# Weight sums of a seven-product matrix multiply: from GpSimd instructions to accumulating DMAs, with the products in another order

## The chip, the cores and the metric

One NeuronCore of a Trainium2 chip runs the whole program, in float32. The metric is the device time of one execution in microseconds (us). TensorE (PE), VectorE (DVE), ScalarE (ACT), GpSimd (POOL) and SyncE (SP) each work through a queue of their own in order and wait for each other on semaphores.

## The reference

The program is three transformer blocks, one after the other, over 512 tokens of width 1024. The change touches only the first mixer, a gated delta-net of 8 heads:

```
proj = h @ w_in                                  # h: 512 x 1024; per head 4 column blocks of 128: q, k, v, z
qkv  = silu(causal_dwconv(q, k, v; 4 taps))
q, k = l2norm(q), l2norm(k)
kk   = strictly lower part of (beta k) k^T * decay
sol  = solve(kk + I, [v*beta, k*beta*exp(gc)])   # in each chunk
scan over chunks: v_new = u - w S;  o = q S + qk v_new;  S = S*decay + k^T v_new
o    = rmsnorm(o) * silu(z);  then o @ w_out
```

## The kernel before

Each head's projection is `W^T H`, with W 1024 x 512 (2 MB, one slot of a ring of three slots in SBUF) and H the 1024 x 512 input, `HT`. It is computed in two pairs of column blocks, p = 0 and p = 1, each by seven half-size products instead of eight. `gdn_quarters(h, p)` gives the four weight quarters A11, A12, A21, A22, each 128 partitions x 512 numbers (256 KB). A11, A12, A22 are also used as they are. Four sums of quarters, S1 to S4, are made in place in the ring slot by four GpSimd instructions for each head and pair (lines 2213, 2220, 2223, 2225; functions `third` and `others`). The four sums of inputs, `gdn_T`, are made once by DVE. The products are called M1 to M7. Each is four matmuls of 128x128 by 128x256; a step of `pe_steps` is one of these (two records in the profile), so a pair has 28 steps and a head 56. All are on line 1467. The order within a pair is M1, M7, M2, M4, M5, M6, M3 (`GDN_ORDER`).

The order of PE is written out by hand. While head h is solved, the steps of head h+1 fill the gaps. `for l in range(1, 7)` are six levels of the triangular inverse. Each level is: LD matmuls (line 1605, level 6: 1607), a few filling steps, TE matmuls (line 1617, level 6: 1619), filling steps, again filling steps; 7 steps in a level. LD of level l needs D of level l-1. TE needs `Tm` (line 2075), which DVE makes from LD; DVE then makes `inv` (lines 2091, 2096) and D (line 2093) from TE. In level 5 four transposes DT (line 1629) stand between the filling steps. After the levels comes a scan over four chunks (lines 1653 to 1670), in which steps 0 to 13 of head h+2 fill (`ahead`). Line 1660 needs the state S of the chunk before, made by DVE (line 2184). So steps 0 to 13 run in the scan two heads ahead, 14 to 27 in levels 1 and 2, 28 to 55 in levels 3 to 6.

DVE has, between its parts of this chain, work that only has to be done in time: convolution taps (line 1906), one eighth of a modulation product in each level (lines 391, 394), the combining additions of the products `t`, `U2`, `c21`, `c22`, `c12` (lines 1919, 1926, 1932, 1937, 1944), and in the scan of head h the first masks of head h+1 (lines 2028, 2032, 2038, 2041). `c12` (line 1944) is the last addition of a pair. ACT copies M1, M7 and M1+M2 out of PSUM (`keep_m1` line 1694, `keep_m7` line 1701, `keep_c11` line 1708) in a fixed place of its queue.

Head 0 has a start of its own: its first steps run while the decays are computed, then kk(0) (line 1516), LT (lines 1523 and 1812), and the first masks; `inv(0, 0)` is ready when DVE ends line 2041.

GpSimd's queue, for each h, is: `third(h+1, 1)`, `third(h+2, 0)`, `others(h+1, 1)`, `scaled(h)` (one 128x512 scaling, line 2249), `decay(h+1)` (two 128x512 products, lines 2231, 2234), `others(h+2, 0)`, `query(h+1)` (line 2243). Before that stands the start, whose end is

```
            third(1, 0)
            decay(0)
            pool.wait_ge(dve_done, at("dve", "gdn", "inv", 0, 0))
            others(1, 0)
            query(0)
```

The ring is loaded by SP: for each head one 2 MB load of a modulation weight (`w_ada`) and one of `w_gdn`, back to back. GpSimd issues no DMA in this kernel.

Of the kernel before, what the change touches and what calls it, by code (L numbers as in the profile page):

```python
# [12 lines left out]
P = 128  # L13
D = 1024
T = 512
# [75 lines left out]
def program(nc, dr, out, plan):  # L91
# [3 lines left out]
    with ExitStack() as ctx:  # L95
# [3 lines left out]
        def sem(name):  # L99
            return ctx.enter_context(nc.semaphore(name))  # L100
# [19 lines left out]
        row_in = sem("row_in")  # L120
        PE, AC, DV, PO = (Steps(plan, e) for e in ("pe", "act", "dve", "pool"))
# [1279 lines left out]
        GDN_ORDER = ("M1", "M7", "M2", "M4", "M5", "M6", "M3")  # L1401
# [15 lines left out]
        def pe_steps(pe, h, s0, s1):  # L1417

            for s in range(s0, s1):
                p, name, k = s // PAIR, GDN_ORDER[s % PAIR // 4], s % 4  # L1420
                A11, A12, A21, A22 = gdn_quarters(h, p)
                Bg, Bx = B[p], B[1 - p]
                if name == "M1":
                    out_, w, x, first = Bg[:, 0:TH], A11, HT[:, 0:4, 0:TH], True
                    if k == 0:
                        if h == 0 and p == 0:
                            pe.wait_ge(first_gdn_in[0], 16)
                        else:
# [3 lines left out]
                elif name == "M7":  # L1432
                    out_, w, x, first = Bx[:, 0:TH], A21, gdn_T[2], True
                    if k == 0:
                        if h == 0:
                            pe.wait_ge(dve_done, at("dve", "gdn", "T3"))
                        if p:
                            pe.wait_ge(dve_done, at("dve", "gdn", "c12", h, 0))
                        elif h:
                            pe.wait_ge(act_done, at("act", "gdn", "z", h - 1))  # L1440
                        pe.wait_ge(pool_done, at("pool", "gdn", "S3", h, p))
                elif name == "M2":
                    out_, w, x, first = Bg[:, 0:TH], A12, HT[:, 4:8, 0:TH], False
                    if k == 0:
                        pe.wait_ge(act_done, at("act", "gdn", "m1", h, p))
                elif name == "M4":
                    out_, w, x, first = Bx[:, 0:TH], A22, gdn_T[3], False
                    if k == 0:
                        if h == 0:
                            pe.wait_ge(dve_done, at("dve", "gdn", "T4"))  # L1450
                        pe.wait_ge(act_done, at("act", "gdn", "m7", h, p))
                elif name == "M5":
                    out_, w, x, first = Bg[:, TH:T], A11, gdn_T[0], True
                    if k == 0:
                        pe.wait_ge(pool_done, at("pool", "gdn", "S1", h, p))
                        if p == 0:
                            pe.wait_ge(act_done, at("act", "gdn", "c11", h))
                elif name == "M6":
                    out_, w, x, first = Bx[:, TH:T], A21, gdn_T[1], True
                    if k == 0:  # L1460
                        pe.wait_ge(pool_done, at("pool", "gdn", "S2", h, p))
                else:
                    out_, w, x, first = Bg[:, TH:T], A12, HT[:, 4:8, TH:T], False
                    if k == 0:
                        pe.wait_ge(pool_done, at("pool", "gdn", "S4", h, p))
# [11 lines left out]
        def pe_gdn(pe):  # L1477
# [96 lines left out]
            for h in range(GH):  # L1574
# [22 lines left out]
                for l in range(1, 7):  # L1597
# [13 lines left out]
                    fill(l, 0, 1)  # L1611
                    pe.wait_ge(dve_done, at("dve", "gdn", "Tm", h, l))
# [68 lines left out]
        def act_gdn(act):  # L1681
# [166 lines left out]
            keep_m7(1, 0)  # L1848
            keep_c11(1)
            lower(0)  # L1850
            for h in range(GH):
                more = h + 1 < GH
                tokens(h)
                if h:
                    oroot(h - 1)
# [12 lines left out]
                if more:  # L1868
                    tap(h + 1, 0)
                    if h:  # L1870
                        keep_m1(h + 1, 1)
                    keep_m7(h + 1, 1)
                    raw(h + 1)
                    silu(h + 1, 1)
                    square(h + 1, 1)
                    silu(h + 1, 0)
                    square(h + 1, 0)
                    roots(h + 1)
                    decays(h + 1)
# [4 lines left out]
                if more:  # L1884
                    gate(h + 1)
                    tap(h + 1, 2)
                    if h + 2 < GH:
                        keep_m1(h + 2, 0)
                        keep_m7(h + 2, 0)
                        keep_c11(h + 2)  # L1890
                    lower(h + 1)
# [18 lines left out]
        def dve_pair(dve, h, p):  # L1910
# [3 lines left out]
            def t():  # L1914

                dve.wait_ge(pe_done, at("pe", "gdn", "M5", h, p))
                dve.wait_ge(act_done, at("act", "gdn", "m7", h, p))
                dve.wait_ge(dve_done, DV.n)
                nc.vector.tensor_tensor(gdn_t, Bg[:, TH:T], gdn_m7, ALU.add).then_inc(dve_done, DV.tick("gdn", "t", h, p))

            def U2():

                dve.wait_ge(pe_done, at("pe", "gdn", "M6", h, p))
                dve.wait_ge(act_done, at("act", "gdn", "m1", h, p))
                dve.wait_ge(dve_done, DV.n)
                nc.vector.tensor_tensor(gdn_U2, Bx[:, TH:T], gdn_m1, ALU.add).then_inc(dve_done, DV.tick("gdn", "U2", h, p))
# [12 lines left out]
            def c12():  # L1939

                dve.wait_ge(pe_done, at("pe", "gdn", "M3", h, p))
                dve.wait_ge(dve_done, DV.n)
                dst = Bg[:, TH:T] if p else raw_q[:, TH:T]
                nc.vector.tensor_tensor(dst, Bg[:, TH:T], gdn_U2, ALU.add).then_inc(dve_done, DV.tick("gdn", "c12", h, p))
# [3 lines left out]
        def dve_gdn(dve):  # L1948
# [4 lines left out]
            nc.vector.tensor_tensor(gdn_T[2], HR[:, 4:8, :], HR[:, 0:4, :], ALU.subtract).then_inc(dve_done, DV.tick("gdn", "T3"))  # L1953
            nc.vector.tensor_tensor(gdn_T[0], HR[:, 0:4, :], HL[:, 0:4, :], ALU.subtract).then_inc(dve_done, DV.tick())
# [7 lines left out]
            nc.vector.tensor_tensor(gdn_T[1], HR[:, 4:8, :], gdn_T[0], ALU.subtract).then_inc(dve_done, DV.tick())  # L1962
# [238 lines left out]
        def pool_gdn(pool):  # L2201
            begin(None, None, "gdn")

            def third(h, p):

                A11, A12, A21, A22 = gdn_quarters(h, p)
                if h == 0:
                    for u in (0, 1) if p == 0 else (2,):
                        pool.wait_ge(first_gdn_in[u], 16)
                if h or p:  # L2210
                    n = load_at[("gdn", h)]
                    pool.wait_ge(ring_full[n % SLOTS], landed(n))
                nc.gpsimd.tensor_tensor(A21, A11, A21, ALU.subtract).then_inc(pool_done, PO.tick("gdn", "S3", h, p))

            def others(h, p):

                A11, A12, A21, A22 = gdn_quarters(h, p)
                pool.wait_ge(pe_done, at("pe", "gdn", "M7", h, p))
                pool.wait_ge(pool_done, at("pool", "gdn", "S3", h, p))
                nc.gpsimd.tensor_tensor(A21, A22, A21, ALU.subtract).then_inc(pool_done, PO.tick("gdn", "S2", h, p))  # L2220
                pool.wait_ge(pool_done, at("pool", "gdn", "S2", h, p))
# [1863 lines left out]
```

## Time and profile before

| | us |
|---|---|
| median of 3 runs | 2595.95 |
| lowest and highest | 2595.76, 2597.06 |
| span of the profiled execution | 2595.1 |
| delta-net stage, about | 40 to 440 of the span |
| one head in the steady part | 47.14 |

For the profiled execution only the span, from its first to its last instruction, is shown; a time of its own beside the span isn't. The span is 0.85 us under the median of the runs. In the groups of rows "idle" in square brackets is the time in which an engine stood still just before the piece, and what ended it. "x8" counts records.

### The profile page before, as it was taken

The numbers are of one execution on the slowest core, as the hardware profiler recorded it, in microseconds if no ns is written. First come the engines' busy times: TensorE is split into PE (matmuls) and PEld (weight loads), VectorE is DVE, ScalarE is ACT, GpSimd is POOL, SyncE is SP. The second block draws the span as 40 slices with busy tenths as digits, with TensorE's granted clock in tenths as the row PEclk, the third lists the DMA queues.
The fourth block names the chain that finished last, engine by engine and source line by source line (L and its number), as shares of the span: only waits on it lengthen the run. The fifth ranks groups of instructions, "written<-read, shape, count | busy, mean of one in ns | idle before, by whom it ended". The sixth has DMA issues, their size and how long they took to land.

```text
span 2595.1 us, 32921 instructions
## 1 busy us (share of the span) xinstructions
PE 2532.1 (98%) x13038; PEld 1999.9 (77%) x13038; DVE 1643.4 (63%) x2905; ACT 719.3 (28%) x1381; POOL 252.9 (10%) x186
## 2 busy tenths in 40 slices
PE   6999999999999999999999999999999999999999
PEld 3777775688888888888888888886445568888888
DVE  2787875687776365455648777745375486666652
ACT  3555553321110122211203111004253375222200
POOL 1434331100000030000001000001121000000000
PEclk9999999999999999999999999999999999999999
DMA  8222311243433321122023453331021310212121
GB/s 350 109 79 74 131 74 72 91 185 146 188 142 144 120 77 70 69 83 84 33 97 130 163 195 148 137 122 69 33 83 65 130 66 33 93 70 98 67 90 55
DMA packets 26377, 276.81 MB, mean 107 GB/s; under 512 B 3689, under 2 KB 4585, under 8 KB 9201
## 3 DMA queue, kind: packets, MB, share of 16 engines
q1 hardware_dynamic: 23040, 268.92, 27.1%
q10 hardware_dynamic: 3184, 5.78, 0.7%
q8 instruction: 105, 1.72, 0.3%
q14 instruction: 48, 0.39, 0.0%
HBM read 272.58 MB, written 2.11 MB: 106 GB/s over the span
## 4 chain that ended last, share of the span: by engine, by line
PE 87%; DVE 7%; ACT 3%; DMA 2%; issue 1%; POOL 0%; SPq 0%; ACTq 0%; DVEq 0%; POOLq 0%
PE bank L688 29%; PE bank L772 15%; PE bank L2583 11%; PE bank L1467 5%; PE bank L2996 5%; PE bank L2369 4%; PE bank L419 3%; DVE arena L1906 1%; PE bank L2674 1%; DMA arena<-w_ada 1%; PE bank L501 1%; PE bank L2989 1%; PE bank L1617 1%; PE bank L1605 1%; PE bank L3139 1%
## 5 line engine op out<-in xcount | busy, mean ns | idle before, releaser
L688 PE MATMUL bank<-HT,ring 128*128 128x256 f32 x1056 | 248.0, 380 | 2.0 <-ACT HT L1104 2.0
L688 PE MATMUL bank<-arena,ring 128*128 128x256 f32 x1056 | 249.5, 379 | 0.0
L688 PE MATMUL bank<-arena 128*128 128x256 f32 x1056 | 249.5, 379 | 0.0
L688 PEld LDWEIGHTS bank<-HT,ring 128*128 128x128 f32 x1056 | 199.3, 190 | 34.2 <-issue 5.2
L688 PEld LDWEIGHTS bank<-arena,ring 128*128 128x128 f32 x1056 | 200.6, 190 | 27.3
L688 PEld LDWEIGHTS bank<-arena 128*128 128x128 f32 x1056 | 200.6, 190 | 27.3
L772 PE MATMUL bank<-arena,ring 128*128 128x256 f32 x936 | 207.0, 379 | 1.4 <-ACT arena L845 1.4
L772 PEld LDWEIGHTS bank<-arena,ring 128*128 128x128 f32 x936 | 177.4, 190 | 27.1 <-ACT arena L845 2.6
L1328 ACT ACTIVATE arena<-bank,ffc 128x512 f32<-128x512 f32 x66 | 51.3, 777 | 487.3 <-DVE bank L1234 487.3
L1133 POOL TENSOR_SCALAR XT<-XT,comb_v 128x512 f32<-128x512 f32 x32 | 50.1, 1577 | 1049.3 <-ACT HT L1104 652.3
L2996 PE MATMUL bank<-HT,ring 128*128 128x512 f32 x320 | 146.5, 598 | 0.5 <-ACT HT L1145 0.5
L1467 PE MATMUL bank<-arena,ring 128*128 128x256 f32 x512 | 133.2, 391 | 2.3 <-DVE arena L1964 0.8
L688 PE MATMUL bank<-HT,arena 128*128 128x256 f32 x528 | 125.5, 381 | 2.5 <-DVE arena L1289 2.4
L772 PE MATMUL bank<-arena 128*128 128x256 f32 x528 | 116.4, 379 | 0.0
L688 PEld LDWEIGHTS bank<-HT,arena 128*128 128x128 f32 x528 | 99.6, 190 | 18.7 <-DVE arena L1289 5.5
L2583 PE MATMUL bank<-arena,ring 128*128 128x256 f32 x512 | 112.7, 379 | 0.3 <-DVE arena L2789 0.3
L772 PEld LDWEIGHTS bank<-arena 128*128 128x128 f32 x528 | 100.3, 190 | 13.6
L2583 PEld LDWEIGHTS bank<-arena,ring 128*128 128x128 f32 x512 | 97.1, 190 | 15.3 <-issue 1.4
L394 DVE SCALAR_TENSOR_TENSOR arena<-ring,evec,arena 128x512 f32<-128x512 f32 x140 | 105.3, 752 | 2.9
L1467 PEld LDWEIGHTS bank<-arena,ring 128*128 128x128 f32 x512 | 90.3, 190 | 17.0 <-DVE arena L1964 1.2
L2996 PEld LDWEIGHTS bank<-HT,ring 128*128 128x128 f32 x320 | 57.2, 190 | 58.9 <-issue 56.8
L1244 DVE SCALAR_TENSOR_TENSOR arena<-bank,ffc,arena 128x511 f32<-128x511 f32 (+1 forms) x132 | 98.5, 746 | 3.5 <-ACT arena L1328 1.1
(509 smaller groups left out, 4403.5 us busy)
## 6 DMA issues: line engine op xcount, KB each, us to landing
ring<-w_ada SPq DMA_DIRECT2D x33, 2048.0 KB, 7.5
ring<-w_up SPq DMA_DIRECT2D x33, 2048.0 KB, 7.4
ring<-w_down SPq DMA_DIRECT2D x24, 1408.0 KB, 6.0
ring<-w_gdn SPq DMA_DIRECT2D x7, 2048.0 KB, 8.9
ring<-w_ret_qk SPq DMA_DIRECT2D x4, 2048.0 KB, 8.2
ring<-w_ret_v SPq DMA_DIRECT2D x4, 2048.0 KB, 8.2
ring<-w_ret_g SPq DMA_DIRECT2D x4, 2048.0 KB, 8.3
ring<-w_ret_out SPq DMA_DIRECT2D x4, 2048.0 KB, 8.3
```

The source lines that it names most:

```text
L394: ins = nc.vector.scalar_tensor_tensor(out=acc, in0=w[:, :, k, :], scalar=evec[:, e, k:k + 1], in1=acc, op0=ALU.mult, op1=ALU.add)
L419: ins = nc.tensor.matmul(B[bank][:, :], out_weights(pe, tag, n, k), src(k), start=(first and k == k0), stop=(last and k == k1 - 1))
L501: last = nc.tensor.matmul(bank[:, cols], out_weights(pe, tag, n, k), HT[:, k, cols], start=(k == 4), stop=(k == KC - 1))
L688: last = nc.tensor.matmul(out_, w[:, k, :], x[:, k, :], start=(first and k == 0), stop=(k == 3), skip_group_check=not first)
L772: last = nc.tensor.matmul(out_, w[:, k, :], x(k), start=(first and k == 0), stop=(k == KH2 - 1), skip_group_check=not first)
L1133: nc.gpsimd.tensor_scalar(XT[:, n, :], XT[:, n, :], comb_v[:, 2, n:n + 1], comb_v[:, 3, n:n + 1], ALU.mult, ALU.add)\
L1244: last = nc.vector.scalar_tensor_tensor(out=out_[:, m:], in0=src[:, 0:T - m], scalar=ffc[:, i, j, half, 2 - m:3 - m], in1=out_[:, m:], op0 ...
L1328: nc.scalar.activation(ffn_y[:, j % 2, :], up_bank(j)[:, :], ACT.Identity, scale=ffc[:, i, j, 0, 2:3], bias=ffc[:, i, j, 0, 3:4])\
L1467: last = nc.tensor.matmul(out_, w[:, k, :], x[:, k, :], start=(first and k == 0), stop=(k == 3), skip_group_check=not first)
L2369: last = nc.tensor.matmul(out_, w[:, k, :], x[:, k, :], start=(first and fresh and k == 0), stop=(k == 7), skip_group_check=not (first and ...
L2583: last = nc.tensor.matmul(out_, left, right, start=flag, stop=(k == 3), skip_group_check=not (first and fresh))
L2996: last = nc.tensor.matmul(bank[:, :], w[:, u, k, :], HT[:, k, :], start=(k == 0), stop=(k == KC - 1))
```

## The change

For heads 1 to 7 the four sums of a pair are made by four DMAs that GpSimd issues with an addition (`accum_op`), each of 256 KB onto a quarter in the ring. Two take their second operand from SBUF (S1, S4), two read the original quarter again from HBM (S3, S2). Since such a DMA is an addition here, the signs of sums and inputs are chosen anew: S1 = A21 + A22, S3 = A11 + A21 (held in A11), S2 = S1 + A11 (held in A21), S4 = A12 + S2. Each sum waits on a semaphore of its own. For head 0 GpSimd still computes the sums by instructions, in a new order and with the new signs.

The order of the products becomes M1, M5, M2, M7, M6, M4, M3. M5 and M3 accumulate in the second half of bank 7 (`gdn_C`), M6 in the second half of the pair's own bank. `pe_ada` (four matmuls with one column) moves for heads 1 to 6 from the end of level 1 to level 3, ahead of TE, and waits there for `c12` of head h+1, pair 0, as it writes bank 7 too. In ACT's queue `keep_c11(0)` and `keep_m7` of the later heads move. `keep_m7(0, 1)` keeps its place.

```diff
-        GDN_ORDER = ("M1", "M7", "M2", "M4", "M5", "M6", "M3")
+        GDN_ORDER = ("M1", "M5", "M2", "M7", "M6", "M4", "M3")
+        gdn_C = B[7][:, TH:T]
...
+                def summed(which):
+
+                    if h:
+                        pe.wait_ge(gdn_sum_in[which][p], 16 * h)
+                    else:
+                        pe.wait_ge(pool_done, at("pool", "gdn", which, h, p))
...
+                    if l == 3 and h and more:
+                        pe.wait_ge(dve_done, at("dve", "gdn", "c12", h + 1, 0))
+                        pe_ada(pe, 0, 3 + h)
                     pe.wait_ge(dve_done, at("dve", "gdn", "Tm", h, l))
...
                     if l == 1 and h and more:
-                        pe_ada(pe, 0, 3 + h)
                         osum(h - 1)
...
+            keep_c11(0)
             keep_m7(0, 0)
             act_root_tables()
             act.wait_ge(act_done, AC.n)
-            keep_c11(0)
...
+            def first_sums(p):
...
+                nc.gpsimd.tensor_tensor(A21, A21, A22, ALU.add).then_inc(pool_done, PO.tick("gdn", "S1", 0, p))
+                pool.wait_ge(pool_done, at("pool", "gdn", "S1", 0, p))
+                pool.wait_ge(pe_done, at("pe", "gdn", "M1", 0, p))
+                nc.gpsimd.tensor_tensor(A11, A11, A21, ALU.add).then_inc(pool_done, PO.tick("gdn", "S2", 0, p))
+                pool.wait_ge(pool_done, at("pool", "gdn", "S2", 0, p))
+                pool.wait_ge(pe_done, at("pe", "gdn", "M5", 0, p))
+                nc.gpsimd.tensor_tensor(A21, A11, A22, ALU.subtract).then_inc(pool_done, PO.tick("gdn", "S3", 0, p))
+                pool.wait_ge(pe_done, at("pe", "gdn", "M2", 0, p))
+                nc.gpsimd.tensor_tensor(A12, A12, A11, ALU.add).then_inc(pool_done, PO.tick("gdn", "S4", 0, p))
+
+            def lower_row(h, p):
...
+                pool.wait_ge(ring_full[n % SLOTS], landed(n))
+                pool.dma_start(flat(A21), flat(A22), accum_op=ALU.add).then_inc(gdn_sum_in["S1"][p], 16)
 
             def others(h, p):
...
                 pool.wait_ge(pe_done, at("pe", "gdn", "M1", h, p))
-                nc.gpsimd.tensor_tensor(A11, A11, A21, ALU.add).then_inc(pool_done, PO.tick("gdn", "S1", h, p))
+                pool.dma_start(flat(A11), in_memory(h, p, 1), accum_op=ALU.add).then_inc(gdn_sum_in["S3"][p], 16)
+                pool.wait_ge(pe_done, at("pe", "gdn", "M5", h, p))
+                pool.wait_ge(gdn_sum_in["S1"][p], 16 * h)
+                pool.dma_start(flat(A21), in_memory(h, p, 0), accum_op=ALU.add).then_inc(gdn_sum_in["S2"][p], 16)
+                pool.wait_ge(gdn_sum_in["S2"][p], 16 * h)
                 pool.wait_ge(pe_done, at("pe", "gdn", "M2", h, p))
-                nc.gpsimd.tensor_tensor(A12, A12, A21, ALU.subtract).then_inc(pool_done, PO.tick("gdn", "S4", h, p))
+                pool.dma_start(flat(A12), flat(A21), accum_op=ALU.add).then_inc(gdn_sum_in["S4"][p], 16)
...
-            third(0, 0)
-            others(0, 0)
-            third(0, 1)
-            others(0, 1)
-            third(1, 0)
+            first_sums(0)
+            first_sums(1)
+            lower_row(1, 0)
             decay(0)
             pool.wait_ge(dve_done, at("dve", "gdn", "inv", 0, 0))
             others(1, 0)
             query(0)
             for h in range(GH - 1):
-                third(h + 1, 1)
+                lower_row(h + 1, 1)
                 if h + 2 < GH:
-                    third(h + 2, 0)
+                    lower_row(h + 2, 0)
                 others(h + 1, 1)
```

## Rows read from the trace of the kernel before

**Rows 1.** The page: busy time, share of the span and instructions of each engine.

```profile
PE 2532.1 (98%) x13038; PEld 1999.9 (77%) x13038; DVE 1643.4 (63%) x2905; ACT 719.3 (28%) x1381; POOL 252.9 (10%) x186
```

**Rows 2.** One head, busy us (count): PE, PEld, DVE, ACT, POOL; clock, DMA share, GB/s.

```profile
211.15:258.29 47.14, 45.17 (x376) 36.16 (x375) 37.98 (x67) 25.43 (x50) 17.59 (x13) 1.00 0.25 96
```

**Rows 3.** The waits of PE between 100 and 400 us: total, times, longest.

```profile
PE bank L1617 <- DVE arena L2075: 7.7, 7, 1.1
PE bank L1660 <- DVE arena L2184: 5.2, 6, 0.9
```

**Rows 4.** Timeline of PE, one head: level 3, level 5, scan.

```profile
192.03 0.68 PE L1617 MATMUL bank<-arena 64*64 64x64 f32 x16
192.64 0.70 PE L1467 MATMUL bank<-HT,ring 128*128 128x256 f32 x2
...
198.25 1.03 PE L1467 MATMUL bank<-arena,ring 128*128 128x256 f32 x4
...
202.49 0.68 PE L1617 MATMUL bank<-arena 64*64 64x64 f32 x16 [1.11 <-DVE arena L2075]
...
222.15 0.49 PE L1660 MATMUL bank<-arena 128*128 128x128 f32 x2 [0.86 <-DVE arena L2184]
...
223.13 0.60 PE L1467 MATMUL bank<-arena,ring 128*128 128x256 f32 x2
```

**Rows 5.** Timeline of DVE in the same head.

```profile
191.45 0.42 DVE L1944 TENSOR_TENSOR arena<-bank,HT 128x256 f32<-128x256 f32 x1
...
199.33 2.77 DVE L1906 SCALAR_TENSOR_TENSOR arena<-arena,gconv 128x511 f32<-128x511 f32 x2
202.02 0.41 DVE L2075 TENSOR_TENSOR arena<-bank,maskL 128x256 f32<-128x256 f32 x1
202.36 0.74 DVE L394 SCALAR_TENSOR_TENSOR arena<-ring,evec,arena 128x512 f32<-128x512 f32 x1
...
219.13 2.58 DVE L2028 TENSOR_TENSOR arena<-arena,maskL 64x256 f32<-64x256 f32 x2
```

**Rows 6.** Timeline of GpSimd in the same head.

```profile
200.51 1.92 POOL L2249 TENSOR_SCALAR XT<-XT 128x512 f32<-128x512 f32 x1
...
218.75 1.27 POOL L2220 TENSOR_TENSOR ring<-ring 128x512 f32<-128x512 f32 x1 [6.26 <-PE bank L1467]
```

**Rows 7.** DVE line 2028 over the stage: shortest, median, longest in ns.

```profile
L2028 DVE TENSOR_TENSOR arena<-arena,maskL x16: 410/1170/1382, 80.6 to 408.3; 64x256 f32<-64x256 f32 x16
```

**Rows 8.** Timeline of PE at the start of head 0.

```profile
66.09 1.89 PE L1467 MATMUL bank<-arena,ring 128*128 128x256 f32 x8
...
78.08 1.16 PE L1516 MATMUL bank<-arena 128*128 128x128 f32 x8 [1.10 <-DVE arena L2004]
...
84.40 1.03 PE L1467 MATMUL bank<-arena,ring 128*128 128x256 f32 x4
...
88.26 2.43 PE L1467 MATMUL bank<-arena,ring 128*128 128x256 f32 x10 [0.54 <-POOL ring L2223]
```

**Rows 9.** Timeline of ACT at the start of head 0.

```profile
63.12 1.28 ACT L1778 ACT_TABLE_LOAD   x1
66.40 0.63 ACT L1778 ACTIVATE arena<-arena 128x512 f32<-128x512 f32 x1 [2.00 <-DVE arena L1906]
...
69.06 0.60 ACT L1757 ACTIVATE arena<-bank 128x512 f32<-128x512 f32 x1 [1.37 <-PE bank L1503]
```

**Rows 10.** Timeline of GpSimd at the start of head 0.

```profile
85.59 1.28 POOL L2220 TENSOR_TENSOR ring<-ring 128x512 f32<-128x512 f32 x1 [8.11 <-DVE arena L2041]
```

**Rows 11.** DMA issues by line: count, KB each, median us from issue to landing.

```profile
ring<-w_gdn SPq DMA_DIRECT2D x7, 2048.0 KB, 8.9
...
arena<-gc_rows ACTq DMA_DIRECT2D x7, 256.0 KB, 3.5
...
arena<-in_ret_D ACTq DMA_DIRECT2D x4, 256.0 KB, 2.6
```

**Rows 12.** Timeline of SP in the head of rows 4: the ring load.

```profile
214.77 0.33 SPq L3847 DMA_DIRECT2D ring<-w_gdn  x1
```

More of the change, by code:

```diff
@@ L120, in program @@
         row_in = sem("row_in")
+        gdn_sum_in = {name: [sem(f"gdn_{name}_in{p}") for p in range(2)] for name in ("S1", "S2", "S3", "S4")}
         PE, AC, DV, PO = (Steps(plan, e) for e in ("pe", "act", "dve", "pool"))
@@ L1431, in pe_steps @@
                             pe.wait_ge(dve_done, at("dve", "gdn", "c21", *pair_before(h, p)))
-                elif name == "M7":
-                    out_, w, x, first = Bx[:, 0:TH], A21, gdn_T[2], True
+                elif name == "M5":
+                    out_, w, x, first = gdn_C, A21, gdn_T[0], True
                     if k == 0:
[L1435 to L1441, printed above, removed]
+                        if h or p:
+                            pe.wait_ge(dve_done, at("dve", "gdn", "c12", *pair_before(h, p)))
+                        else:
+                            pe.wait_ge(dve_done, at("dve", "gdn", "T1"))
+                        summed("S1")
                 elif name == "M2":
@@ L1445, in pe_steps @@
                         pe.wait_ge(act_done, at("act", "gdn", "m1", h, p))
+                elif name == "M7":
+                    out_, w, x, first = Bx[:, 0:TH], A11 if h else A21, gdn_T[2], True
+                    if k == 0:
+                        if h == 0:
+                            pe.wait_ge(dve_done, at("dve", "gdn", "T3"))
+                        if h and p == 0:
+                            pe.wait_ge(act_done, at("act", "gdn", "z", h - 1))
+                        summed("S3")
+                elif name == "M6":
+                    out_, w, x, first = Bg[:, TH:T], A21 if h else A11, gdn_T[1], True
+                    if k == 0:
+                        if h == 0:
+                            pe.wait_ge(dve_done, at("dve", "gdn", "T4"))
+                        if p == 0:
+                            pe.wait_ge(act_done, at("act", "gdn", "c11", h))
+                        summed("S2")
                 elif name == "M4":
@@ L1448, in pe_steps @@
                     if k == 0:
-                        if h == 0:
-                            pe.wait_ge(dve_done, at("dve", "gdn", "T4"))
                         pe.wait_ge(act_done, at("act", "gdn", "m7", h, p))
-                elif name == "M5":
-                    out_, w, x, first = Bg[:, TH:T], A11, gdn_T[0], True
+                else:
+                    out_, w, x, first = gdn_C, A12, HT[:, 4:8, TH:T], False
                     if k == 0:
[L1455 to L1465, printed above, removed]
+                        summed("S4")
                         pe.wait_ge(dve_done, at("dve", "gdn", "t", h, p))
@@ L1847, in act_gdn @@
             tap(0, 2)
-            keep_m7(1, 0)
             keep_c11(1)
@@ L1853, in act_gdn @@
                 tokens(h)
+                if more:
+                    keep_m7(h + 1, 0)
                 if h:
@@ L1871, in act_gdn @@
                         keep_m1(h + 1, 1)
-                    keep_m7(h + 1, 1)
                     raw(h + 1)
@@ L1875, in act_gdn @@
                     square(h + 1, 1)
+                    keep_m7(h + 1, 1)
                     silu(h + 1, 0)
@@ L1888, in act_gdn @@
                         keep_m1(h + 2, 0)
-                        keep_m7(h + 2, 0)
                         keep_c11(h + 2)
@@ L1918, in t @@
                 dve.wait_ge(dve_done, DV.n)
-                nc.vector.tensor_tensor(gdn_t, Bg[:, TH:T], gdn_m7, ALU.add).then_inc(dve_done, DV.tick("gdn", "t", h, p))
+                nc.vector.tensor_tensor(gdn_t, gdn_m7, gdn_C, ALU.subtract).then_inc(dve_done, DV.tick("gdn", "t", h, p))
             def U2():
@@ L1925, in U2 @@
                 dve.wait_ge(dve_done, DV.n)
-                nc.vector.tensor_tensor(gdn_U2, Bx[:, TH:T], gdn_m1, ALU.add).then_inc(dve_done, DV.tick("gdn", "U2", h, p))
+                nc.vector.tensor_tensor(gdn_U2, Bg[:, TH:T], gdn_m1, ALU.subtract).then_inc(dve_done, DV.tick("gdn", "U2", h, p))
             def c21():
@@ L1943, in c12 @@
                 dst = Bg[:, TH:T] if p else raw_q[:, TH:T]
-                nc.vector.tensor_tensor(dst, Bg[:, TH:T], gdn_U2, ALU.add).then_inc(dve_done, DV.tick("gdn", "c12", h, p))
+                nc.vector.tensor_tensor(dst, gdn_C, gdn_U2, ALU.subtract).then_inc(dve_done, DV.tick("gdn", "c12", h, p))
             return t, U2, c21, c22, c12
@@ L1952, in dve_gdn @@
             dve.wait_ge(dve_done, at("dve", "gdn", "input", 6))
-            nc.vector.tensor_tensor(gdn_T[2], HR[:, 4:8, :], HR[:, 0:4, :], ALU.subtract).then_inc(dve_done, DV.tick("gdn", "T3"))
-            nc.vector.tensor_tensor(gdn_T[0], HR[:, 0:4, :], HL[:, 0:4, :], ALU.subtract).then_inc(dve_done, DV.tick())
+            nc.vector.tensor_tensor(gdn_T[0], HL[:, 0:4, :], HR[:, 0:4, :], ALU.subtract).then_inc(dve_done, DV.tick("gdn", "T1"))
+            nc.vector.tensor_tensor(gdn_T[2], HR[:, 0:4, :], HR[:, 4:8, :], ALU.subtract).then_inc(dve_done, DV.tick("gdn", "T3"))
             nc.vector.memset(reset[0:GH, :], 1.0).then_inc(dve_done, DV.tick())
@@ L2202, in pool_gdn, with flat @@
             begin(None, None, "gdn")
-            def third(h, p):
-                A11, A12, A21, A22 = gdn_quarters(h, p)
[L2207 to L2213, printed above, removed]
+            def flat(quarter):
+                return quarter.rearrange("p k n -> p (k n)")
@@ new lines, in in_memory @@
+            def in_memory(h, p, n):
+                c = GDN_UNITS[p][n] * KC * P
+                return dr["w"]["gdn"][h][:, c:c + 4 * P]
+            def first_sums(p):
+                A11, A12, A21, A22 = gdn_quarters(0, p)
+                for u in (0, 1) if p == 0 else (2,):
+                    pool.wait_ge(first_gdn_in[u], 16)
+                if p:
+                    n = load_at[("gdn", 0)]
+                    pool.wait_ge(ring_full[n % SLOTS], landed(n))
[8 more added lines that the diff above has]
+                nc.gpsimd.tensor_tensor(A12, A12, A11, ALU.add).then_inc(pool_done, PO.tick("gdn", "S4", 0, p))
@@ L2215, in others @@
+            def lower_row(h, p):
+                A11, A12, A21, A22 = gdn_quarters(h, p)
+                n = load_at[("gdn", h)]
+                pool.wait_ge(ring_full[n % SLOTS], landed(n))
+                pool.dma_start(flat(A21), flat(A22), accum_op=ALU.add).then_inc(gdn_sum_in["S1"][p], 16)
             def others(h, p):
                 A11, A12, A21, A22 = gdn_quarters(h, p)
-                pool.wait_ge(pe_done, at("pe", "gdn", "M7", h, p))
-                pool.wait_ge(pool_done, at("pool", "gdn", "S3", h, p))
```

4 lines of the change are left out of this document (1 added, 3 removed).

## The prediction

> **What bounds the kernel now.** I read the page first: PE is busy in 98% of the span [rows 1], so only what shortens PE's own queue, or its waits, can shorten the program. The change adds and removes no matmul. Next, the busy times by stretch, cut from one ring load to the next, which is one head: 47.14 us, of which PE is busy 45.17 at full granted clock, DVE 37.98 and GpSimd 17.59 [rows 2]. So a head has 1.97 us of idle PE. That is the most that a head of the steady part can give back, some 14 us in seven heads. The list of PE's waits says where it is: 7 times before line 1617, 7.7 us together, and 6 times before line 1660, 5.2 us together [rows 3]. In the timeline of a head they are 1.11 us at level 5, and 0.86 us at the last chunk of the scan [rows 4].
>
> Both waits are for DVE, and both come from DVE instructions that take longer than they need beside a GpSimd instruction. Ahead of `Tm` of level 5 two taps take 2.77 us, and ahead of the state S two masks take 2.58 us [rows 5]. The second stretch begins at 219.13, when GpSimd is in the sum of line 2220 from 218.75 on [rows 6]. The same mask takes 410 ns at its shortest and 1170 at its median [rows 7]; two undisturbed ones would be 0.82 us, so 1.76 us are lost in waiting for GpSimd. The Trainium skill states the cause (SBUF — State Buffer, "SBUF: two separate sides"): DVE with two SBUF operands and GpSimd take a shared port pair by turns, for the whole instruction. The two durations agree.
>
> PE never waits for the sums themselves in the steady part; it does so once at the start of head 0, 0.54 us [rows 8].
>
> **The change part by part.** *The GpSimd sums of heads 1 to 7 go.* The 0.54 us in head 0 go with them: 0.5 gained. At level 5, the two taps undisturbed are over some 1.3 us earlier (2.77 less two of about 0.75, which is the 0.74 of line 394's like instruction in [rows 5]). `Tm` then is ready before the three filling steps end, and the wait of 1.11 goes. But `scaled(h)` stays; it holds DVE off from 200.51 for 1.92 us, and line 394 could start only at 202.36 [rows 5, 6]. If it starts where it did, the next `inv` is ready where it was, and the transposes DT behind it wait half a microsecond or so; then only 0.5 us is gained. If it starts after line 394, the whole 1.1. Its start now depends on when S2 lands. I take the middle, 0.8, seven times: 5.6 us; the ends are 3.5 and 7.7. In the scan, the masks are freed and S is ready 1.7 us earlier, so the 0.86 goes, if no new wait stands in its place.
>
> *The DMAs take their place.* I need the time L from GpSimd's issue to landing, and no row has an accumulating DMA or one of GpSimd. Nearest are 256 KB transfers of the ACT queue: 2.6 us from HBM, 3.5 for a broadcast row [rows 11]. The 2 MB load of 8.9 us says that 256 KB more cost about (8.9 - 2.6) / 7 = 0.9 us, and an accumulating transfer has to read its destination too: 3.5 to 4.4. I take 4.2, near the upper one, as GpSimd's own part in issuing isn't in it. From below it is bounded by 2.6, from above by the 8.9 of a load eight times as large.
>
> The Trainium skill (DMA: Bandwidth & Descriptors, "Anatomy of one DMA — SWDGE (gpsimd) path") would have a DMA from GpSimd take 2.0 us plus its bytes by 436 GB/s; its estimate for 256 KB is 2.6 us, which would make the sum below 1.6 us lower. No row here shows it for an accumulation. Against the change speaks the other page (SBUF — State Buffer, "SBUF: two separate sides"): GpSimd writes descriptors for such DMAs into SBUF, and is locked out while DVE runs in a two-port mode, so that a DMA seems blocked. No run so far has such a DMA, and nothing in the sum is taken from it.
>
> *Does L fit?* Pair 1: M1 (steps 28 to 31) ends at 193.2. M7 is now steps 40 to 43, and step 40 is the third piece of level 4, at 198.25 [rows 4]. S3 has 5.0 us. S2, from the end of M5 (step 35, about 195.7) to step 44 (about 200.8), has as much. With L = 4.2 neither waits. Pair 0: S3 goes out when M1 ends at about 215.9 (GpSimd began at 218.75 four steps of products and two scan matmuls later, [rows 6]). M7 begins with step 12 at 223.13 [rows 4], or 0.86 earlier once that wait is gone: 6.4 us. But in that time the ring load of 2 MB issued at 214.77 is in flight, to about 223.7 [rows 11, 12]. The engines are shared, and no row shows two queues side by side. From below the delay is nothing (4.2 against 6.4); from above S3 lands with the load, some 1.4 us too late, which would more than eat the 0.86. I take half of the gain: 6 x 0.43 = 2.6 us; the ends are 5.2 and -3.
>
> *The new order of products* costs PE nothing in the steady part. M6 and M4 have their inputs (`keep_m7` of pair 0 runs behind `tokens`, some 2 us before step 20 needs it, and that of pair 1 behind `square`, well ahead of step 48). The pieces of pe_ada move from level 1 to level 3 with their 0.8 us of PE. Its new wait for `c12`: that ended at 191.87 [rows 5], and TE followed at 192.03 [rows 4]; the levels before come 0.8 us earlier for PE and DVE alike, so the wait is met. If DVE were late there, TE, `inv` and LD of level 4 would follow.
>
> *Head 0 pays.* First, `keep_m7(0, 1)` keeps its place in ACT's queue, ahead of the table load and the silu of k. M7(0, 1) was done ahead of the table load at 63.12 [rows 9], but is now the product that ends at 66.09 + 1.89 = 67.98 [rows 8]. Behind it come its own copy 0.36, the table load 1.28, the silu 0.63 [rows 9] and a square as long: 70.9. There line 1757, which began at 69.06 [rows 9], can start: 1.9 us late. From there ACT runs without a gap to `khat`, for which PE already waits 1.10 us at 78.08 [rows 8]. So the 1.9 us fall on PE in full. Softplus, behind M7(0, 0) now, adds some 0.2 us.
>
> Second, steps 12 and 13 of head 1, at 84.40 [rows 8], used to be M4; now they are M7 and need S3(1, 0). That DMA stands behind the wait for `inv(0, 0)` in GpSimd's queue, which was met at 85.59 [rows 10]. Both moments shift by the 1.9 us. PE stands still for 85.59 - 84.40 + L = 1.2 + 4.2 = 5.4 us, once. Queued behind step 12 is level 1 of head 0, and so DVE's chain; nothing else can use the time.
>
> *Sum:* gains 0.5 + 5.6 + 2.6 = 8.7; losses 1.9 + 0.2 + 5.4 = 7.5; net -1.2. The span of 2595.1 becomes 2593.9. For the profiled execution nothing is shown beside its span, and the median stands 0.85 above it: 2594.8 us.
>
> **The rivals.** *Faster:* the relief of DVE counts in full. 7.7 + 5.2 + 0.5 = 13.4 gained, and with L = 3.5 head 0 loses 6.8: -6.6, so 2589.4. For it: the waits are the same in every head, and the DMAs leave DVE's port alone. Against: the ring load in flight at every S3 of pair 0.
>
> *Slower:* L exceeds the 5.0 us that pair 1 has. Each microsecond over it costs 7 us, one for each head from 1 to 7, at step 40, with level 5 queued behind. At L = 6 that is 7 us, plus 1.8 more in head 0, and pair 0 waits about 1 us in 6 heads and gives nothing back (+2.6): -1.2 + 7 + 1.8 + 2.6 = +10.2, plus up to 6 for pair 0. That is 2606 to 2612. It is the slower side by over 0.2% from L = 5.4 or so, if pair 0 gives nothing. For it: software makes the descriptors, three streams of 256 KB instead of two, a second of two DMAs on the same queue. Against: 2.6 and 3.5 us for plain ones.
>
> *No relief:* GpSimd, in issuing a DMA, holds DVE off as long as a sum did (1.3 us). Then nothing is gained at either wait, and head 0 costs 7: +7, 2603. A milder form, a third of it, is within the forecast.
>
> **How the numbers follow.** About 0.2% (5.2 us) is what a measurement of this kernel can tell from no change. My forecast, 2591 to 2600, has 0.44; the faster rival 0.30; late DMAs 0.18; no relief 0.08. So faster 0.30, same 0.44, slower 0.26. The range leaves out one in ten on each side: down to 2587 (all 13.4 gained, head 0 losing 5) and up to 2606 (L = 6 with pair 0 in time).
>
> **What would show it.** Right: PE's waits before line 1617 on line 2075 gone or halved; two of line 2028 at 0.82 us; a gap of some 5 us ahead of a line-1467 piece at 86 us, ended by the DMA, and 3 us ahead of line 1516; ring loads less than 46.5 us apart. Wrong: new gaps ahead of steps 40 or 44, or step 12, ended by a ring DMA in every head; issue of a DMA by GpSimd to landing over 5 us; masks still at 1.2 us; or a head 0 without its gap, which would be 5 us better than I say.

## The result, and the profile after

The changed kernel takes 2627.8 us (median of 4 runs, 2624.05 to 2629.95), against 2596.5 for the kernel before in as many: a ratio of 1.0118, with a 95% interval from 1.0105 to 1.0131. It is 31 us slower, where 1.2 us faster was forecast, and it lies outside the predicted range. The profiled span is 2624.3 us, 29.2 longer. The change's stage has nearly all of that: the load that closes it, the first of `w_gdn_out`, is issued at 428.56 instead of 399.85.

First, the page's busy times:

```profile
span 2624.3 us, 32935 instructions
PE 2545.6 (97%) x13038; PEld 2012.2 (77%) x13038; DVE 1604.2 (61%) x2905; ACT 719.8 (27%) x1381; POOL 219.5 (8%) x186
```

GpSimd and DVE are less busy [rows 1], so the sums did leave GpSimd. Next, what PE waits for from 40 to 450 us (us in total, times, longest):

```profile
PE bank L1479 <- DMA ring<-w_gdn: 28.0, 7, 5.6
PE bank L1528 <- DVE arena L2018: 2.9, 1, 2.9
PE bank L1674 <- DVE arena L2195: 1.4, 1, 1.4
```

Both repeated waits of [rows 3] are gone, 7.7 and 5.2 us in total. In their place stand 7 waits of the products for a GpSimd DMA (line 1479 is the line of all products, 1467 before). PE's timeline shows where, with start, duration, and in brackets the idle time ahead and what ended it:

```profile
80.00 2.08 PE L1528 MATMUL bank<-arena 128*128 128x128 f32 x8 [2.93 <-DVE arena L2018]
93.51 2.04 PE L1479 MATMUL bank<-arena,ring 128*128 128x256 f32 x4 [5.57 <-DMA ring<-w_gdn]
...
140.42 0.67 PE L1479 MATMUL bank<-arena,ring 128*128 128x256 f32 x2 [3.60 <-DMA ring<-w_gdn]
...
190.62 0.67 PE L1479 MATMUL bank<-arena,ring 128*128 128x256 f32 x2 [3.54 <-DMA ring<-w_gdn]
```

The first two are head 0, to which 3.0 and 5.4 us were given. The others come in each of the six heads that follow, ahead of step 12, M7 of pair 0; four more are of 3.58 to 4.46 us. The six make 22.4 us. What ends them is the landing of S3 of pair 0. GpSimd's issues (line 2256 is S3, 2259 S2, 2262 S4) and SP's in the same heads:

```profile
130.92 0.90 POOL L2256 DMA_DIRECT2D ring<-w_gdn  x1 [3.80 <-PE bank L1674]
...
181.19 0.90 POOL L2256 DMA_DIRECT2D ring<-w_gdn  x1 [3.79 <-PE bank L1674]
183.89 0.86 POOL L2259 DMA_DIRECT2D ring<-w_gdn  x1 [1.80 <-PE bank L1674]
192.04 0.86 POOL L2262 DMA_DIRECT2D ring<-ring  x1 [7.29 <-DMA ring<-w_gdn]
```

```profile
125.80 0.33 SPq L3882 DMA_DIRECT2D ring<-w_ada  x1
129.41 0.33 SPq L3882 DMA_DIRECT2D ring<-w_gdn  x1
...
179.68 0.33 SPq L3882 DMA_DIRECT2D ring<-w_gdn  x1
```

SP issues the 2 MB load 1.5 us ahead of S3, and S3 lands just before step 12 starts at 140.42: after 9.4 us, counted from its issue. In the six heads it takes 9.3 to 10.4 us, and always lands 0.5 to 0.6 us behind the load. S2 of pair 0, issued 2.7 to 2.9 us behind S3, is late too, 7.9 to 8.9 us; no product waits for it. In pair 1, with no load in flight, S3 takes 4.1 to 4.2 us (4.6 in head 1) and S2 4.0 to 4.3. The view of S3's line, with both pairs in it:

```profile
DMA to landing us min/median/max: 4.1/4.4/10.4
```

The DMA issues of the stage by what they move (KB of each, median us to landing; in the last line fast and slow ones are mixed):

```profile
ring<-w_gdn SPq DMA_DIRECT2D x6, 2048.0 KB, 10.3
ring<-ring POOLq DMA_DIRECT2D x28, 256.0 KB, 3.7
ring<-w_gdn POOLq DMA_DIRECT2D x28, 256.0 KB, 4.5
```

The load, for its part, takes 10.3 us instead of 8.9 [rows 11].

The waits aren't all. Windows from one `w_ada` load to the next, as in [rows 2] (us, then PE, PEld, DVE, ACT, POOL busy with their instructions, PE's granted clock, DMA share, GB/s):

```profile
125.80:176.06 50.26, 46.66 (x376) 37.60 (x375) 31.59 (x66) 25.43 (x50) 12.74 (x13) 0.97 0.55 147
176.06:224.66 48.60, 45.06 (x376) 36.29 (x376) 32.10 (x67) 25.36 (x50) 12.72 (x13) 1.00 0.51 136
224.66:274.98 50.32, 46.67 (x376) 37.58 (x376) 32.19 (x67) 25.43 (x50) 12.72 (x13) 0.97 0.49 132
```

The middle head is the clean case: PE has no idle time left but the gap, 45.06 + 3.54 = 48.60. In the heads beside it the same 376 matmuls take 1.6 us more, and the granted clock is 0.97. The windows right behind two of the gaps, PE alone (us, busy, clock, DMA share, GB/s), place the loss:

```profile
141.00:146.00 5.00, 5.00 (x37) 0.66 0.81 195
...
192.00:197.00 5.00, 5.00 (x53) 1.00 0.62 105
```

After one gap the granted clock falls for some microseconds towards the lower of its two levels; after another of the same length, it doesn't. In the first case eight matmuls of line 1543 take 1.78 us, in the second 1.06:

```profile
141.14 1.78 PE L1543 MATMUL bank<-arena 128*128 128x128 f32 x8
...
191.35 1.06 PE L1543 MATMUL bank<-arena 128*128 128x128 f32 x8
```

So the account of the six heads from 125.80 to 428.56 is: 302.8 us against 6 x 47.14 = 282.8, which is 19.9 more. The gaps are 22.4; what is beyond 45.06 and the gap in each head, read as the clock, is 10.0 (two heads lose 1.6, one 1.8, two 2.5); relief gives 6 x (47.14 - 45.06) = 12.5 back. The remaining 8.8 of the stage lie ahead, in head 0 and the start of head 1: 5.6 for the first S3 and 1.8 more for `khat` (2.93 against 1.10), less 0.5 of the GpSimd wait and 1.1 of a level 5, leave some 3 us. There too matmuls behind gaps run at half the rate (the eight of line 1528, the products of keys with keys, take 2.08 us at 80.00 and 1.06 elsewhere); that this makes the 3 us isn't shown.

### The profile page after: what moved, and what is told of

Same layout as the page of the kernel before. It is cut to its first block, busy times and chain, and to the rows that moved or that the text cites. A ratio compares the mean times of both kernels' runs of the same rounds, so it can differ in the third digit from the quotient of the medians.

```text
span 2624.3 us, 32935 instructions
## 1 busy us (share of the span) xinstructions
PE 2545.6 (97%) x13038; PEld 2012.2 (77%) x13038; DVE 1604.2 (61%) x2905; ACT 719.8 (27%) x1381; POOL 219.5 (8%) x186
## 4 chain that ended last, share of the span: by engine, by line
PE 86%; DVE 4%; ACT 3%; DMA 3%; issue 2%; SPq 1%; POOL 1%; ACTq 0%; POOLq 0%; DVEq 0%
PE bank L689 30%; PE bank L773 15%; PE bank L2618 11%; PE bank L1479 5%; PE bank L3031 5%; PE bank L2404 4%; PE bank L420 3%; DMA ring<-w_gdn 3%; PE bank L2709 1%; PE bank L502 1%; PE bank L3024 1%; PE bank L1617 1%; PE bank L1632 1%; PE bank L3174 1%; PE bank L2700 1%
## 6 DMA issues: line engine op xcount, KB each, us to landing
ring<-w_gdn SPq DMA_DIRECT2D x7, 2048.0 KB, 10.3
```

## The experiments

Every kernel was timed against the kernel before on its own chip, whose medians were 2596.1 to 2596.8 us. The theories: A, S3 of pair 0 queues behind the bytes of the 2 MB load that is issued just ahead of it; B, a DMA of GpSimd is slow by itself in that stretch (its descriptors, or DVE's work beside it).

**The load later.** SP holds the `w_gdn` loads of heads 3 to 7 until S2 of pair 0 has landed:

```
  if key[0] == "gdn" and key[1] >= 3:
      sp.wait_ge(gdn_sum_in["S2"][0], 16 * (key[1] - 1))
```

> Change: the kernel after, but SP holds back the 2 MB load of w_gdn (heads 3 to 7) until S2 of the pair 0 that is just being summed has landed; the load of w_ada ahead of it is not held. Theory A (S3 of pair 0 is late because it shares the DMA engines with the ring loads): S3 issues some 5 us after the w_ada load, overlaps it for about 2.5 us and lands 5 to 6.5 us after issue instead of 9.4; the gap of 3.6 us ahead of M7 shrinks to under 0.7 in five heads, the clock stays at 1.0 there, the program takes 2598 to 2604. Theory B (the DMA is late because GpSimd cannot write its descriptors while DVE runs in the scan): landing and gap as in the kernel after, about 2628.

Measured: 2600.1 us, 1.0017 [1.0007, 1.0027]. PE's waits in the stage:

```profile
PE bank L1479 <- DMA ring<-w_gdn: 9.2, 2, 5.6
...
PE bank L1479 <- DMA ring<-ring: 1.4, 3, 0.8
```

The 9.2 are head 0's 5.6 and 3.6 in head 7, whose load, a second `w_ada`, wasn't held. The held ones have no gap and no slow matmuls behind it, with GpSimd's DMAs, their number and DVE's work the same:

```profile
136.86 0.60 PE L1479 MATMUL bank<-arena,ring 128*128 128x256 f32 x2
...
137.51 1.06 PE L1543 MATMUL bank<-arena 128*128 128x128 f32 x8
```

S3 of these five heads lands after 4.1 to 4.4 us, as in pair 1, though the last 2.3 to 2.5 us of the `w_ada` load are still in flight beside it; I had expected 5 to 6.5. S4, which now goes out 0.3 us behind the held load, takes 9.4 to 10.3 us in its turn and lands 0.6 to 0.7 us behind it. It reads no HBM, so its lateness isn't that of a read from there. That is theory A, and B is out. One wait on SP gives some 27 us back.

**Both loads later.** The `w_ada` load that goes out 3.6 us ahead of the other is held too (`key[:2] == ("ada", 0) and 5 <= key[2] <= 10`, for the same semaphore).

> Change: as the run before, but SP holds back the w_ada load of the same head as well, so that no ring load is in flight beside S3 and S2 of pair 0. Theory A: S3 lands in 4.4 us as in pair 1, no gap ahead of M7, but both loads start 12 us later; DVE may wait up to 1 us for w_ada in level 1. 2597 to 2602. Theory B: gap stays 3.6 us, about 2628.

Measured: 2630.8 us, 1.0136 [1.0121, 1.0151]: a miss. S3 landed in 4.1 to 4.3 us and its gap was gone, but `w_ada`, issued at 137.87, is what DVE's modulation product (line 392) needs some microseconds later, and behind that in DVE's queue stands what PE waits for (line 2023). DVE's timeline, and PE's waits:

```profile
146.65 0.49 DVE L392 TENSOR_SCALAR arena<-ring,evec 128x512 f32<-128x512 f32 x1 [5.14 <-DMA ring<-w_ada]
```

```profile
PE bank L1571 <- DVE arena L2023: 28.4, 6, 5.3
PE bank L1479 <- DMA ring<-w_gdn: 5.7, 1, 5.7
```

I had priced the late `w_ada` at no more than 1 us. Of two loads that stand in the way, only the one that isn't needed soon can be moved.

**The load in pieces.** The two loads of 16 KB in each partition are cut in four DMAs of 4 KB, or in eight of 2 KB:

```
  for u in range(4):      # 8 in the second kernel
      c = slice(u * (SLOT // 4), (u + 1) * (SLOT // 4))
      sp.dma_start(ring[:, n % SLOTS, c], src[:, c]).then_inc(ring_full[n % SLOTS], 16)
```

> Change: the kernel after, with each ring load beside the delta-net heads cut into four DMAs of 4 KB per partition instead of one of 16 KB. Theory A1 (the engines take turns between queues by whole pieces of a load, and each 2 KB piece of the sum waits behind a 16 KB piece): S3 lands in 5 to 7 us, the gap falls to under 1.2 us, 2600 to 2610. Theory A2 (what counts is the bytes of the ring load still to move, or HBM): S3 lands in 9 us as before and the time is that of the kernel after, 2628 or a little more for the longer issue.

> Change: the kernel after with each ring load of the delta-net heads cut into eight DMAs of 2 KB per partition, the piece size of the sums. Cutting into four brought the landing of S3 from 9.4 to some 8.4 us. If turns by pieces were the main cause, this brings it to 7 or less and the gaps under 1 us: 2600 or less. If it is the queue's bytes and the engines' full load, it stays at 8 us and over: 2608 to 2615.

Measured: 2611.2 us, 1.0060 [1.0045, 1.0075], and 2610.4, 1.0053 [1.0039, 1.0066]. With four pieces the gaps of five heads are 2.3 to 2.8 us and that of the last, whose load is a second `w_ada` and wasn't cut, is 4.4; with eight, 1.0 to 2.4 and 4.6. S3's landing in the five heads falls from 9.3 to 10.4 us to between 8.1 and 8.6 with four pieces, and to between 7.8 and 8.1 with eight, 6.8 in one head. (Issuing in eight pieces keeps SP itself busy for 3.65 us with the first load and 4.9 to 6.9 with the second, so that part of the load is issued behind S3.) Smaller pieces let S3 through sooner, but far from in proportion; that the rest of the delay is the bytes ahead is an argument, not shown.

The gaps of the six heads fall from 22.4 to 17.0 us with four pieces, and the time by 16.6 in the medians. Most of what is left between them is the clock: in the five heads with gaps of 2.3 to 2.8 us PE is busy for 45.1 to 45.2 us at full granted clock, in the sixth for 47.35 at 0.93. The first and the sixth:

```profile
126.37:174.27 47.90, 45.06 (x376) 36.33 (x375) 31.60 (x66) 25.37 (x50) 12.76 (x13) 1.00 0.58 154
...
364.44:416.15 51.71, 47.35 (x376) 38.22 (x375) 32.09 (x67) 25.44 (x50) 11.86 (x12) 0.93 0.47 123
```

With eight pieces it fell again in two of the five, behind gaps of 2.1 and 1.9 us (46.7 and 46.9 us busy). So the length of a gap alone doesn't say whether the clock falls.

**Pair 0 by GpSimd.** Only pair 1's sums by DMA; pair 0's as before, by GpSimd instructions, with the new order of products.

> Change: the sums of pair 0 of every head are GpSimd instructions again (in the new order and signs), those of pair 1 stay DMAs. Theory A: gaps ahead of M7 of pair 0 gone; the wait of 0.86 us for S in the scan is back, that of 1.1 us at level 5 stays away; head 0 waits 3 to 4 us for S3 instead of 5.6. 2594 to 2600. If instead the DMAs or the order cost something that is not these gaps, it stays above 2605.

Measured: 2601.1 us, 1.0022 [1.0012, 1.0031]. That is 1 us above the expected range. There is no wait for a DMA in a steady head; the waits for DVE are back, and not only the expected one in the scan (line 1682) but half of that at level 5 too (line 1632):

```profile
PE bank L1682 <- DVE arena L2184: 5.9, 7, 0.9
PE bank L1479 <- POOL ring L2264: 3.8, 1, 3.8
PE bank L1632 <- DVE arena L2089: 2.7, 5, 0.5
```

**The order alone.** All sums by GpSimd, the products in the new order.

> Change: the new order of products, banks, signs and places in ACT's queue, but all sums of all heads by GpSimd instructions. What the order alone costs: head 0 some 1.9 + 3.8 us and a little clock, otherwise as before the change: 2600 to 2606. If the moved pe_ada or the copies delay the chain in every head: over 2610.

Measured: 2603.8 us, 1.0033 [1.0020, 1.0046]. The reordering alone costs 7.5 us, of which 5.1 is in head 0 (3.8 for a sum of GpSimd where it was 0.54, 2.9 for `khat` where it was 1.1); the waits for DVE stay, at 7.3 and 6.4 us. A steady head takes 47.38 us, 0.24 more than before; the cause of that wasn't looked for.

**The start alone.** In head 0, GpSimd doesn't wait for `inv(0, 0)` before S3(1, 0), and ACT copies M7 behind its square:

```
-            keep_m7(0, 1)
             silu(0, 1)
             square(0, 1)
+            keep_m7(0, 1)
...
             decay(0)
-            pool.wait_ge(dve_done, at("dve", "gdn", "inv", 0, 0))
             others(1, 0)
```

> Change: the kernel after with the start of head 0 mended: GpSimd no longer waits for inv(0, 0) before it issues S3(1, 0), and ACT copies M7(0, 1) after the square of k instead of before the silu. By the prediction's terms: 1.9 us ahead of line kk(0) come back, and of the 5.6 us gap most; but S3(1, 0) now issues at 79 us, beside the ring load of 75.4 to 84, so 1 to 3 us of gap may stay. With the clock 2618 to 2623. If these two places were not the cause of head 0's loss: 2628.

Measured: 2618.5 us, 1.0079 [1.0062, 1.0096]: some 9 us less than the change. `khat` is awaited for 1.1 us again, head 0's gap is gone (S3(1, 0), beside the ring load, takes 6.7 us, and there is time for it), and the six others stay (23.0 us in all).

**Work in the gap.** Seven matmuls more, of no use, ahead of the wait for S3, to tell waiting from the clock. Step 12 can't start sooner by them.

```
  for j in range(7):
      nc.tensor.matmul(out_, A22[:, j % 4, :], x[:, j % 4, :], start=True, stop=True)
  summed("S3")
```

> Change: the kernel after, with seven more matmuls of 128x128 by 128x256 on PE in front of the wait for S3 of pair 0, heads 1 to 7, into the PSUM half that M7 overwrites next; their results are not used. They take 3.3 us, so they fill the gaps of 3.6 us and change nothing else. Theory C (each gap lets the granted clock fall, and the matmuls after it run at half of it: about 10 us of the 31 lost are this, not the waiting): the clock stays at 1.0, 2615 to 2620. Rival (the clock in the rows costs nothing that the gaps don't): 2627 to 2631.

Measured: 2620.9 us, 1.0097 [1.0082, 1.0113]. PE does more, and the whole is shorter by 6.9 us in the medians and 5.5 in the ratios, whose intervals overlap a little. S3 lands even later than before, after 10.2 to 10.7 us (the loads beside it take longer too, 11.0 to 11.9; why isn't known). An idle 1.3 to 1.9 us is left of each gap in the six heads:

```profile
135.04 3.19 PE L1462 MATMUL bank<-arena,ring 128*128 128x256 f32 x14
139.97 0.70 PE L1481 MATMUL bank<-arena,ring 128*128 128x256 f32 x2 [1.75 <-DMA ring<-w_gdn]
...
140.73 1.06 PE L1545 MATMUL bank<-arena 128*128 128x128 f32 x8
```

The same eight matmuls took 1.78 us behind the longer gap. To part the waiting from the clock, I cut each head at step 12. From there to the next `w_ada` load PE has the same 300 matmuls in both kernels and no idle time. The first two heads with the filler, and then without it (the change):

```profile
139.97:174.05 34.08, 34.08 (x300) 26.32 (x301) 21.79 (x43) 20.36 (x42) 9.70 (x10) 1.00 0.38 75
189.96:225.63 35.67, 35.67 (x300) 27.60 (x301) 21.76 (x43) 20.43 (x42) 9.63 (x10) 0.95 0.29 53
```

```profile
140.42:176.06 35.64, 35.64 (x300) 27.57 (x301) 21.77 (x43) 20.43 (x42) 9.65 (x10) 0.95 0.38 76
190.62:224.66 34.04, 34.04 (x300) 26.29 (x301) 21.76 (x43) 20.36 (x42) 9.63 (x10) 1.00 0.33 58
```

Over the six heads these stretches take 206.3 us with the filler (five of 34.1 to 34.3, one of 35.67) and 214.1 without it (one of 34.04, five of 35.6 to 36.6). Six of 34.04 would be 204.2. So the filler gives 7.8 us of the clock's 9.8 back, and the later step 12, 4.9 us in the same heads, hides most of that. That a gap costs more than its length is shown, and its size, some 10 us, too.

**No sums at all.** The kernel before, with the weight sums of heads 1 to 7 left out. It shows what is left when the sums cost nothing.

> Change: the kernel before (old order) with the weight sums of heads 1 to 7 left out, so that M1 to M7 of these heads use unsummed quarters and the output is not the reference's. It shows what freeing GpSimd and DVE is worth by itself. By the waits of before: 7.7 + 5.2 + 0.5 us less, 2582 to 2585. If the waits before lines 1617 and 1660 have another cause than GpSimd's sums: 2590 or more.

Measured: 2581.4 us, 0.9941 [0.9927, 0.9954]. Both DVE waits of [rows 3] are gone, and the time is 0.6 us below the expected range:

```profile
159.46:204.30 44.84, 44.84 (x376) 36.26 (x375) 33.28 (x67) 25.45 (x50) 5.98 (x5) 1.00 0.26 101
```

A head is 44.84 us with PE never idle. That is 2.3 less than 47.14, not 1.97: PE's busy time of 45.17 in [rows 2] held 0.3 us that no view had named.

**Put together.** The start mended, and the `w_gdn` loads of heads 2 to 7 and the last `w_ada` held, first until S2 of pair 0 has landed, then until S4 has:

```
  if key[0] == "gdn" and key[1] >= 2 or key == ("ada", 0, 11):
      sp.wait_ge(gdn_sum_in["S2"][0], 16 * (key[1] - 1 if key[0] == "gdn" else 7))   # then "S4"
```

> Change: the kernel after with the w_gdn loads of heads 2 to 7 and the last w_ada load held back until S2 of pair 0 in flight has landed, and with the start of head 0 mended as in the run with only that. Theory A: no gap of over 1 us is left in heads 1 to 7, both DVE waits of before are gone, and head 0 costs nothing: 2583 to 2588, faster than both kernels. If something else than these waits held the kernel: over 2594.

> Change: as the best version so far, but the loads are held until S4 of pair 0 has landed, not S2. In the run with S2 the S4 that goes out at the same time as the load lands 9.7 us later in head 0 and M3 waits 2.9 us there and 0.2 to 0.5 in the other heads. Expected: those 4.7 us go, and no new wait comes, as the load, now 3.5 us later, is wanted by GpSimd only 8 us before its next work: 2583 to 2586. If the later load makes GpSimd late for S3 of pair 1: 2588 or more, with gaps in level 4.

Measured: 2588.2 us, 0.9970 [0.9961, 0.9979], with S2, at the upper edge of what was expected. What is left there is S4, issued just as the held load starts:

```profile
PE bank L1479 <- DMA ring<-ring: 4.7, 6, 2.9
```

With S4: **2581.6 us**, 0.9944 [0.9930, 0.9957], less than both kernels, below the expected range, and level with no sums at all. SP's two loads in one head, and the window of that head:

```profile
159.67 0.33 SPq L3883 DMA_DIRECT2D ring<-w_ada  x1
175.99 0.33 SPq L3883 DMA_DIRECT2D ring<-w_gdn  x1
```

```profile
159.67:204.50 44.83, 44.83 (x376) 36.27 (x376) 34.06 (x67) 25.38 (x50) 12.92 (x13) 1.00 0.58 148
```

The load goes out 16.3 us behind `w_ada` instead of 3.6, and nothing waits for it.

## Why the prediction was wrong

**The step that failed** is pair 0 in "Does L fit?": "I take half of the gain: 6 x 0.43 = 2.6 us; the ends are 5.2 and -3." The danger was seen there (the ring load in flight, no row with two queues side by side), but its upper end was too low. I let S3 land with the load "some 1.4 us too late" by taking the load's 8.9 us [rows 11] as fixed. That S3 lands with the load, the upper end, was what came in all six heads, and it was priced too low: the load slowed to 10.3, 1.4 us more, and S3 landed another 0.5 to 0.6 us behind it. So S3 took 9.3 to 10.4 us, when some 6 were there: 3.5 to 4.5 us late in each head, 22.4 us in place of the 2.6 gained. Holding the load took the gaps away in the five heads where it was held (2600.1) with GpSimd's DMAs as they were, so the cause is shown. Two of the prediction's own signs of being wrong had named it: gaps ahead of step 12, ended by a ring DMA, and landings over 5 us. The Trainium skill (DMA: Bandwidth & Descriptors, "Issuing engines are not separate DMA queues") says that DMAs of all engines run on the same 16 DMA engines and interleave. The trace agrees that DMAs of SP and GpSimd delay each other: 4.2 us alone, 9.4 beside 2 MB.

**A term that was missing:** what a gap does to TensorE's clock. The rows of before showed 1.00 throughout a head [rows 2], and I took a microsecond of waiting to cost a microsecond. Here the same matmuls took about 10 us more in the six heads, at a granted clock of 0.93 to 0.97 in five of them. Two experiments bear this out: with useless matmuls in the gaps the stretches behind them were 7.8 us shorter, and with the load in four pieces five of the six heads were at full clock again.

**Point by point, the other terms.**

- *DVE's relief* was right in mechanism and low in size. Two masks take 0.86 us instead of 2.58, two taps 1.53 instead of 2.77 [rows 5]:

```profile
184.04 0.86 DVE L2042 TENSOR_TENSOR arena<-arena,maskL 64x256 f32<-64x256 f32 x2
...
213.54 1.53 DVE L1920 SCALAR_TENSOR_TENSOR arena<-arena,gconv 128x511 f32<-128x511 f32 x2
```

  Both waits went in full, 1.11 and 0.86 us in a head, where 0.8 and 0.43 were taken. With the order alone they stayed, so it is GpSimd's sums that made them, as said. The two masks at 184.04 run while GpSimd issues S2 (183.89, 0.86 us) and are no longer for it: *no relief* is refuted.
- *L* was right where no load is in flight: 4.0 to 4.3 us for S3 and S2 of pair 1 (the sums that read `w_gdn` again; 4.6 once), 3.2 to 3.9 for S4 and S1 (slot to slot; 4.5 once, and 4.6 to 5.2 for an S1 issued right behind another), with 4.2 taken. *Pair 1* was in time in every head; the *slower* rival had the right mechanism, a late S3, but put it there, and its 10 to 16 us were half of what came, or less.
- The lockout of GpSimd's DMAs by DVE that the prediction cited (the Trainium skill, SBUF — State Buffer, "SBUF: two separate sides") wasn't seen: L was about 4.2 us with DVE busy 32.10 us of 48.60. Whether DVE was ever in a two-port mode beside such an issue, no run shows. By the Trainium skill's estimate (DMA: Bandwidth & Descriptors, "Anatomy of one DMA — SWDGE (gpsimd) path"), 2.6 us, L would be 1.6 us too short; the measurement decides.
- *Head 0* was sized right: 2.93 for 3.0 at `khat`, 5.57 for 5.4 at S3(1, 0). The start mended gave 9.3 us back, more than the 7.3 of the two terms; matmuls at half rate behind those gaps may be the difference, which isn't shown.
- *The order* costs little in the steady part: nothing to be seen in a head of the change, whose PE was idle only in the gap, and 0.24 us a head in the run with the order alone. `c12` was in time.
- The *faster* rival's relief of 13.4 us was real, even low (the kernel without sums is 15 us faster than before); what it lacked was the load out of the way.

**Open:** how the 16 DMA engines divide their turns between the two queues. A small DMA issued up to 1.5 us behind an uncut load landed 0.5 to 0.7 us behind it, but 2.3 to 3.3 behind where a second load followed the first at once (S4 with both loads held); pieces of 4 and 2 KB made that 8.1 to 8.6 and mostly 7.8 to 8.1 us, which neither equal turns nor first come, first served explains by itself. Why the clock falls behind one gap and not behind another isn't settled either: it stayed at 1.00 behind one of 3.54 us in the change, and fell behind one of 1.87 with the filler.

## What to carry to other kernels

Before work is given to a DMA that something waits for, list every large load that is in flight between its issue and its need, on any queue. If the load is issued just ahead of it, price the small transfer at the end of the large one, lengthened by their sharing; if that doesn't fit, move the load that isn't needed soon, by a wait ahead of it on the issuing queue until the last of the small ones has landed. Read what the load's consumer needs before holding it: of two loads ahead of S3, one could go 12.7 us later at no cost, and holding the other cost 31 us. And price a gap on TensorE above its length: here 22.4 us of gaps cost 10 more.

## What was new of the hardware

- An accumulating 256 KB DMA issued by GpSimd lands after 4.0 to 4.3 us where it reads from HBM and 3.2 to 3.9 from slot to slot (a few single ones up to 5.2), and takes GpSimd 0.9 us to issue, an S1 1.0 to 1.5. Issued 1.5 us behind a 2 MB load it lands after 9.3 to 10.4 us, 0.5 to 0.6 behind the load, which takes 10.3 us instead of 8.9. Beside a load that was issued 5.1 us earlier and ends 2.3 us later, it is hardly slower (4.1 to 4.4).
- Cutting the load in smaller DMAs shortens the small one's delay by far less than in proportion (pieces of 16, 4, 2 KB in a partition: 9.3 to 10.4, 8.1 to 8.6, and 7.8 to 8.1 us, once 6.8).
- After a gap of 3.6 to 4.5 us the granted clock was 0.51 to 0.66 over the next 5 us in five heads, which cost 1.6 to 2.5 us each, and after one of 3.54 us it stayed at 1.00. With shorter gaps it fell three times, behind 1.86, 1.87 and 2.14 us, and stayed up behind seven of 2.3 to 2.8 us.
